# Gate and up products by Strassen's seven block products, with GpSimd making the weight sums

## The chip, the cores and the metric

The kernel runs on one core of a Trainium2 chip, as one program. The metric is the device time of one execution in microseconds. The core's engines run side by side and are ordered by semaphores alone: TensorE (PE, matmuls, with its weight loads as a row of their own), VectorE (DVE), ScalarE (ACT), GpSimd (POOL) and SyncE (SP), whose queue issues the loads from memory. Each engine works through its own list of instructions in order.

## What is computed

Two transformer layers, then one block of another kind, over 512 tokens of width 1024 in float32. Each of the three ends in a gated feed-forward part (FFN) with 2816 hidden features; only that part is touched:

```python
for l in range(DEPTH):                       # 2 layers
    ...                                      # attention; x = x + mix @ w_o[l]
    xn = _rms_norm(x, ffn_norm[l])
    gate, up = jnp.split(xn @ w_gate_up[l], 2, axis=-1)
    x = x + (jax.nn.silu(gate) * up) @ w_down[l]
...                                          # second block, with w_ffn_in, w_ffn_out:
x = x + g2 * _swiglu(_modulate(_rms_norm_2(x, norm2_g[i]), sh2, sc2), w_ffn_in[i], w_ffn_out[i])
```

## The kernel before

**Precision by parts.** Every float32 operand of a large product is split into a rounded high part and the rest, the low part, both in the format that TensorE reads at full rate. A product is three passes: high by high, high by low, low by high. High parts are made by ScalarE copies (`split_high`, line 1865, for weights), low parts by VectorE subtractions (`split_low`, line 2447). All matmuls are issued by one helper, so they carry line 865.

**One FFN** (`ffn`, line 1152). Features are on the partitions. The 2816 hidden features are 22 tiles of 128 (`FT`). For tile q < 22, the weights' columns of gate and up, 1024 x 128 each, are loaded as two transfers of 512 KB into one of two raw buffers, `raws[:, g % 2]` (line 1570); ScalarE copies the 2048 columns to `wH[:, g % 2]`, VectorE subtracts to `wL[:, g % 2]`. TensorE runs 8 contraction tiles x 3 passes for gate into one bank of PSUM, and as many for up into another: 48 matmuls that read 512 columns each. For q from 22 on, 16 halves of the down projection follow: 11 hidden tiles x 3 passes, 33 matmuls of 512 columns, with 1408 weight columns to load and split. The load of piece g waits until the low part of piece g-2 is made (line 1566), so two pieces are on their way at any time.

**Between gate and down** (`scaled_products`, line 2401, for the two layers): VectorE multiplies the gate's bank by the inverse norm (line 2404), ScalarE takes SiLU (line 1890), VectorE multiplies by the up bank (2408), splits the next weights, scales again (2411) and at once splits the hidden tile into `hH` and `hL` (2440, 2441). In the second block the norm is applied ahead of the products and the two scalings fall away (`ffn_products`, ScalarE reads the gate's bank).

**Stream tiles.** While the output projection's eight tiles come out of PSUM, VectorE adds each to `xT`, applies the gain and splits it with ScalarE into `xH`, `xL`, so that the first gate products can follow at once.

**Conditioning.** Beside the two layers' FFNs, GpSimd weighs and folds 64 pieces of `w_ada` of 512 KB (`conditioning`, lines 735 to 749), one for each step q = 0 to 31; SyncE loads each behind the weights of step q+1 (line 1580), TensorE transposes it at the end of step q (`modulation`), ScalarE reads it out.

Of the kernel before, what the change touches and what calls it, by code (L numbers as in the profile page):

```python
# [20 lines left out]
FF = 2816  # L21
# [60 lines left out]
def build(nc, A, out):  # L82
    ctx = ExitStack()
    with ctx:
# [85 lines left out]
        xH = sb("xH", [P, KT, S], FR)  # L170
        xL0 = sb("xL0", [P, KT // 2, S], FR)
        hH = sb("hH", [P, FT, S], FR)
        hL = sb("hL", [P, FT, S], FR)
        xL1 = sb("xL1", [P, KT // 2, S], FR)
        kept = sb("kept", [P, 2048])
        FP = 2 * KT * P
        raws = sb("raws", [P, 2, FP])
        wH = sb("wH", [P, 2, FP], FR)
        wL = sb("wL", [P, 2, FP], FR)
        sb("spare_held", [P, 2, KT * P])  # L180

# [49 lines left out]
        def wo_parts(e):  # L231

            n, home = WO_ROWS * P, WO_HOMES[e]
            a = home * 2 * n if home < 4 else (18816, 6656)[home - 4]
            raw_, parts_ = (ring_flat, ring_parts_flat) if home < 4 else (R, R_parts)
            return [t.rearrange("p (k c) -> p k c", k=WO_ROWS)
                    for t in (raw_[:, a:a + n], parts_[:, a + n:a + 2 * n], parts_[:, a:a + n])]

# [140 lines left out]
        ADA_FIRST, N_ADA = 0, len(ADA) // L  # L379
# [19 lines left out]
        ctx_root, ctx_inverse, ctx_split = sem("ctx_root"), sem("ctx_inverse"), sem("ctx_split")  # L399
        sq_ready, folded = sem("sq_ready"), sem("folded")  # L400
        sums_full, spread_full, inv_copied = sem("sums_full"), sem("spread_full"), sem("inv_copied")
        token_inv_ready, lat_eps_ready = sem("token_inv_ready"), sem("lat_eps_ready")
        gate_full, gate_scaled = sem("gate_full"), sem("gate_scaled")
# [27 lines left out]
        silu_ready, silu_used = sem("silu_ready"), sem("silu_used")  # L431
# [4 lines left out]
        cs_ready, mod_ready = sem("cs_ready"), sem("mod_ready")  # L436
# [204 lines left out]

        ysb = U[:, :, :].rearrange("p a c -> p (a c)")[:, 0:TT * D].rearrange("p (t c) -> p t c", t=TT)
# [5 lines left out]
        def _(pool):  # L648
# [160 lines left out]
            pool.wait_ge(wl_ready, L * NF)  # L809
# [35 lines left out]
            pg.seen[folded] = 2 * L * (KT - 2)  # L845
            fold_squares()


        @block.tensor
        def _(pe):  # L850
# [54 lines left out]
            def stream_sums(l):  # L905

                if l > 0:
                    pe.wait_ge(inv_copied, l)
# [243 lines left out]
            def ffn(l):  # L1152
# [3 lines left out]
                else:  # L1156
                    folded_sums(X(0), X(KT - 1))
                    spread_roots(S)

                def gate_bank(q):  # L1160
                    n = l * FT + q
                    if n >= 2:
                        pe.wait_ge(gate_scaled, n - 1)
                    return A_BANKS[q % 2]
# [11 lines left out]
                xl = lambda k: (xL0 if k < KT // 2 else xL1)[:, k % (KT // 2), :]  # L1176
                for q in range(NF):
                    g = l * NF + q
                    pe.wait_ge(wl_ready, g + 1)
                    if l == L and q == 0:  # L1180
                        w = [[(lambda k, t=t, n=n: t[:, g % 2, (n * KT + k) * P:(n * KT + k + 1) * P]) for t in (wH, wL)] for n in range(2)]
                        banks = [ab.fill(pe), db.fill(pe)]
                        for k in range(KT):
                            pp.more(xn_ready)
                            both = [products(banks[n][:, :], w[n], lambda k: xH[:, k, :], xl, [k], k == 0, k == KT - 1) for n in range(2)]
                        both[0].then_inc(a_full, 1)
                        both[1].then_inc(d_full, 1)
                        f_by.append((d_full, db.n))
                    elif q < FT:
                        for n, b_ in ((0, ab), (1, db)):  # L1190
                            w = [(lambda k, t=t: t[:, g % 2, (n * KT + k) * P:(n * KT + k + 1) * P]) for t in (wH, wL)]
                            deferred = l < L and n == 0
                            bank = gate_bank(q) if deferred else b_.fill(pe)
                            products(bank[:, :], w, lambda k: xH[:, k, :], xl, list(range(KT)), True, True,
                                     (lambda k: pp.more(xn_ready)) if q == 0 and n == 0 else None
                                     ).then_inc(gate_full if deferred else b_.filled, 1)
                            if l < L and q == 0:
                                if n == 0:
                                    stream_sums(l)
                                else:  # L1200
                                    pp.more(diag_ready)
                                    mm(NB[:, :], ones[:, :], dg[:, :], True, True).then_inc(spread_full, 1)
                        f_by.append((d_full, db.n))
# [1641 lines left out]
```

## Time and profile before

| | |
|---|---|
| time, median of 2 | 2747.14 us (2746.83 to 2747.44) |
| the profiled execution | 2746.26 us, of which the span of the profile is 2744.5 |
| TensorE busy | 2597.4 us (95%) |
| VectorE busy | 1413.8 us (52%) |
| ScalarE busy | 1011.3 us (37%) |
| GpSimd busy | 850.8 us (31%) |
| chain that ended last | TensorE 80%, VectorE 11%, ScalarE 5% |
| memory read | 226 MB, 83 GB/s over the span |

A busy share is an average over stages. In the chain's row the shares are of the span, followed back from the last instruction. A matmul's duration in the trace (0.39 us for 512 columns) is its way through the array; matmuls overlap, and what one costs is the distance from its start to the next one's.

### The profile page before, as it was taken

The numbers are of one execution on the slowest core, as the hardware profiler recorded it, in microseconds if no ns is written. First come the engines' busy times: TensorE is split into PE (matmuls) and PEld (weight loads), VectorE is DVE, ScalarE is ACT, GpSimd is POOL, SyncE is SP. The second block draws the span as 40 slices with busy tenths as digits, with TensorE's granted clock in tenths as the row PEclk, the third lists the DMA queues.
The fourth block names the chain that finished last, engine by engine and source line by source line (L and its number), as shares of the span: only waits on it lengthen the run. The fifth ranks groups of instructions, "written<-read, shape, count | busy, mean of one in ns | idle before, by whom it ended". The sixth has DMA issues, their size and how long they took to land.

```text
span 2744.5 us, 35667 instructions
## 1 busy us (share of the span) xinstructions
PE 2597.4 (95%) x13916; PEld 2151.6 (78%) x13916; DVE 1413.8 (52%) x1863; ACT 1011.3 (37%) x1732; POOL 850.8 (31%) x654
## 2 busy tenths in 40 slices
PE   7998999999999988999999899997998999899998
PEld 6976778888899667888888688876876788688887
DVE  2848664454427487654443445557555633534332
ACT  5448722222334487222222344453233200222222
POOL 5467534434435476334444110032000112000000
PEclk9999999999999999999999999998999999999999
DMA  5321034444432100345545121211112234233322
GB/s 127 87 54 23 11 91 130 139 138 139 135 95 88 49 16 11 106 123 147 145 128 155 46 50 47 57 37 46 47 47 54 67 95 123 62 93 92 93 87 82
DMA packets 396711, 230.47 MB, mean 84 GB/s; under 512 B 9744, under 2 KB 392848, under 8 KB 396544
## 3 DMA queue, kind: packets, MB, share of 16 engines
q1 hardware_dynamic: 394608, 226.19, 29.2%
q0 software_dynamic: 1936, 2.00, 0.9%
q8 instruction: 111, 1.82, 0.3%
q14 instruction: 56, 0.46, 0.1%
HBM read 226.07 MB, written 2.10 MB: 83 GB/s over the span
## 4 chain that ended last, share of the span: by engine, by line
PE 80%; DVE 11%; ACT 5%; issue 2%; DMA 1%; POOL 0%; DVEq 0%; SPq 0%; ACTq 0%; POOLq 0%
PE ps L865 70%; PE scores L865 8%; DVE R L2224 1%; PE ps L1009 1%; DVE ring_parts L2500 1%; DVE spare L2234 1%; DMA ring<-in_w_in 1%; DVE wL L2447 1%; DMA R<-in_x 0%; DVE R L2676 0%; ACT R L1731 0%; DVE QK_parts L2214 0%; ACT spare L1726 0%; DVE R L2677 0%; PE scores L937 0%
## 5 line engine op out<-in xcount | busy, mean ns | idle before, releaser
L865 PE MATMUL ps<-xH,wH 128*128 128x512 f32 x1000 | 395.7, 396 | 6.8 <-DVE xL L2420 4.6
L865 PE MATMUL ps<-xH,wL 128*128 128x512 f32 x1000 | 390.8, 391 | 0.0
L865 PE MATMUL ps<-xL,wH 128*128 128x512 f32 x1000 | 390.7, 391 | 0.0
L1865 ACT ACTIVATE wH<-raws 128x2048 fp32r<-128x2048 f32 (+1 forms) x114 | 193.0, 1693 | 465.2 <-PE ps L865 381.4
L865 PE MATMUL ps<-ring_parts,U_parts 128*128 128x256 f32 (+2 forms) x2000 | 328.9, 291 | 27.9 <-DVE ring_parts L2500 14.2
L2447 DVE TENSOR_TENSOR wL<-raws,wH 128x2048 fp32r<-128x2048 f32 (+1 forms) x114 | 237.8, 2086 | 188.6 <-ACT wH L1865 187.2
L865 PEld LDWEIGHTS ps<-ring_parts,U_parts 128*128 128x128 f32 x2000 | 289.9, 197 | 36.0 <-DVE ring_parts L2500 15.4
L865 PE MATMUL ps<-R 128*64 128x128 f32 (+4 forms) x1538 | 224.2, 318 | 31.3 <-DVE R_parts L2245 7.0
L742 POOL TENSOR_TENSOR spare<-spare,cvec 128x1024 f32<-128x1024 f32 x64 | 123.9, 1935 | 400.9 <-DMA spare<-in_w_ada 400.8
L817 POOL CAST ring_parts<-ring 128x2048 fp32r<-128x2048 f32 x34 | 65.6, 1929 | 569.3 <-DMA ring<-in_w_in 500.3
L865 PE MATMUL ps<-U_parts,ring_parts 128*128 128x512 f32 (+2 forms) x768 | 228.2, 386 | 6.7 <-DVE ring_parts L2500 6.7
L865 PEld LDWEIGHTS ps<-R 128*128 128x128 f32 (+1 forms) x1538 | 162.9, 166 | 86.9 <-issue 38.8
L865 PEld LDWEIGHTS ps<-xH,wH 128*128 128x128 f32 x1000 | 188.6, 189 | 52.8 <-issue 5.2
L865 PEld LDWEIGHTS ps<-xH,wL 128*128 128x128 f32 x1000 | 188.6, 189 | 40.1
L865 PEld LDWEIGHTS ps<-xL,wH 128*128 128x128 f32 x1000 | 188.6, 189 | 37.8
L865 PE MATMUL ps<-hH,wH 128*128 128x512 f32 x528 | 208.3, 394 | 0.0
L865 PE MATMUL ps<-hH,wL 128*128 128x512 f32 x528 | 206.0, 390 | 0.0
L865 PE MATMUL ps<-hL,wH 128*128 128x512 f32 x528 | 205.6, 389 | 0.0
L746 POOL TENSOR_TENSOR spare<-spare 128x512 f32<-128x512 f32 (+1 forms) x168 | 170.7, 1016 | 13.2
L865 PEld LDWEIGHTS ps<-U_parts,ring_parts 128*128 128x128 f32 (+1 forms) x768 | 139.8, 186 | 40.7 <-DVE ring_parts L2500 8.1
L712 POOL TENSOR_TENSOR ring_parts<-ring,ring_parts 128x2048 fp32r<-128x2048 f32 (+2 forms) x23 | 99.7, 4337 | 164.8 <-ACT ring_parts L1651 164.5
L865 PE MATMUL ps<-ring_parts 128*128 128x512 f32 (+1 forms) x400 | 137.6, 344 | 0.0
(450 smaller groups left out, 4712.0 us busy)
## 6 DMA issues: line engine op xcount, KB each, us to landing
raws<-in_w_gate_up SPq DMA_DIRECT2D x88, 512.0 KB, 5.2
ring<-in_w_in SPq DMA_DIRECT2D x34, 1024.0 KB, 6.0
spare<-in_w_ada SPq DMA_DIRECT2D x64, 512.0 KB, 3.8
raws<-in_w_down SPq DMA_DIRECT2D x32, 704.0 KB, 5.6
raws<-in_w_ffn_in SPq DMA_DIRECT2D x44, 512.0 KB, 5.1
ring<-in_w_in SPq DMA_DIRECT2D x26, 512.0 KB, 5.4
raws<-in_w_ffn_out SPq DMA_DIRECT2D x16, 704.0 KB, 4.5
ring<-in_w_o SPq DMA_DIRECT2D x12, 448.0 KB, 3.7
```

The source lines that it names most:

```text
L712: pg.do(nc.gpsimd.tensor_tensor(low, slot(i, KT, n_), high.bitcast(F32), ALU.subtract), piece_low)
L742: pg.do(nc.gpsimd.tensor_tensor(w_, w_, bc(cvec[:, :, ADA[a][1]], P, 2), ALU.mult))
L746: pg.do(nc.gpsimd.tensor_tensor(w[:, 0:n_ * P], w[:, 0:n_ * P], w[:, n_ * P:2 * n_ * P], ALU.add), ada_summed if n_ == left else None)
L817: pg.do(nc.gpsimd.tensor_copy(high, raw_), second_high)
L865: return nc.tensor.matmul(o, a, b, start=first, stop=last)
L1009: ins = nc.tensor.transpose(bank[:, s_ * P:(s_ + 1) * P], PX[a % 4][:, c, s_ * P:(s_ + 1) * P], ident[:, :])
L1865: ap.do(f(wH[:, g % 2, 0:n], raws[:, g % 2, 0:n], ACT.Copy), wh_ready)
L2224: vp.do(v.tensor_reduce(nmax[:, n:n + 2], SP[a % 2][:, :, :], AX.X, ALU.max, negate=True), s_max)
L2234: vp.do(v.scalar_tensor_tensor(px[:, 0, :], px[:, 1, :], ratio[:, 0:1], px[:, 0, :], ALU.mult, ALU.add), combined)
L2447: vp.do(v.tensor_tensor(wL[:, g % 2, 0:n], raws[:, g % 2, 0:n], wH[:, g % 2, 0:n].bitcast(F32), ALU.subtract), wl_ready)
L2500: vp.do(v.tensor_tensor(low, raw_, high.bitcast(F32), ALU.subtract), piece_split)
```

## The change

The contraction (1024) is halved, the tokens (512) are halved, and the output side is the pair (gate, up): a 2 x 2 by 2 x 2 block product, done with seven block products (Winograd's form) of 128 x 512 weights by 512 x 256 activations in place of eight. Each block product has 4 contraction tiles x 3 passes, 84 matmuls of 256 columns a hidden tile.

- The weights' blocks A11, A12 (gate), A21, A22 (up, called S3 and A22 when they land) come by four loads of 256 KB into one landing area, `landing`, 3584 columns, of which the loads fill four blocks of 512. GpSimd makes S1, S2, S4 and S3 there by four operations of 512 columns (`weight_sums`). ScalarE copies a first group of four blocks (2048 columns) and a second group of three (1536); VectorE subtracts 2048, then 1024 and 512. The parts are held twice, the landing area once: a tile's loads wait for `lows_made(l, q - 1)`, both low groups of the tile before.
- The activations' sums (T1 to T4) are made by VectorE in the two layers and by GpSimd in the second block (`stream_differences`), and split as before.
- The seven products go to four banks, three pairs of them adding up in place. ScalarE copies product 1 out (`copy_first`); VectorE puts the sums together (`first_sums`, `gate_tile`, `hidden_tile`).
- Hidden tiles are kept whole; they are split all together during the last tile, for want of room (`hidden_high`, `hidden_low`).
- Conditioning moves two steps later (`ADA_FIRST` from 0 to 2), and GpSimd does it between the sums. Some semaphores are merged.

```diff
+        landing = ring_flat[:, 0:7 * QW]
+        FIRST_GROUP, SECOND_GROUP = ("A11", "S3", "S1", "S2"), ("A12", "A22", "S4")
+        def lows_made(l, q):
+            return l * (2 * FT + 2 * KT) + (2 * q + 2 if q < FT else FT + q + 1)
+        H_TURNS = ((0, 7, 4), (7, 12, 7 + 2), (12, 17, 7 + 4), (17, 19, 7 + 5), (19, FT, 7 + 6))
+        PRODUCTS = (("A11", "B11"), ("S1", "T1"), ("S2", "T2"), ("S3", "T3"), ("A12", "B21"), ("S4", "B22"), ("A22", "T4"))
-        ADA_FIRST, N_ADA = 0, len(ADA) // L
+        ADA_FIRST, N_ADA = 2, len(ADA) // L
...
+            def weight_sums(l, j):
+                w = full_part
+                pool.wait_ge(raw_in[0], weights_landed(l, j))
+                for dst, a, b, op in (("S1", "S3", "A22", ALU.add), ("S2", "S1", "A11", ALU.subtract),
+                                      ("S4", "A12", "S2", ALU.subtract), ("S3", "A11", "S3", ALU.subtract)):
+                    pg.do(nc.gpsimd.tensor_tensor(w[dst], w[a], w[b], op), sums_made if dst == "S3" else None)
             def conditioning(l):
                 pool.wait_ge(cs_ready, 1)
+                for j in range(ADA_FIRST + 2):
+                    weight_sums(l, j)
                 for a in range(l * N_ADA, (l + 1) * N_ADA):
...
+                    if a - l * N_ADA + ADA_FIRST + 2 < FT:
+                        weight_sums(l, a - l * N_ADA + ADA_FIRST + 2)
...
+                    for a_, b_, end in ((wh, xh, False), (wh, xl_, False), (wl, xh, i == KH - 1)):
+                        ins = nc.tensor.matmul(o, a_, b_, start=begin, stop=end, skip_group_check=goes_on)
...
+                        pe.wait_ge(wl_ready, lows_made(l, q) - 1)
+                        if q >= 2:
+                            pe.wait_ge(h_made, n - 1)
...
+                        pe.wait_ge(wl_ready, lows_made(l, q))
+                        pe.wait_ge(first_taken, n + 1)
+                        for m in range(4, 7):
+                            if m == 5:
+                                pe.wait_ge(fifth_taken, n + 1)
...
-                    if q >= 2:
-                        sp.wait_ge(wl_ready, g - 1)
+                        if q >= 1:
+                            sp.wait_ge(wl_ready, lows_made(l, q - 1))
+                        for half, gate, up in ((0, "A11", "S3"), (1, "A12", "A22")):
+                            for a, name in enumerate((gate, up)):
+                                sp.dma_start(full_part[name].rearrange("p (k c) -> p k c", k=KH),
...
+            def weights_room(l, j, products_of_two_ago):
+                if j >= 2:
+                    act.wait_ge(quad_full, 7 * (l * FT + j - 2) + products_of_two_ago)
...
+                act.wait_ge(sums_made, l * FT + j + 1)
...
                 for q in range(NF):
                     if q < FT:
+                        if q + 1 < FT:
+                            second_group_high(l, q + 1)
                         else:
+                            split_high(l, FT)
+                        if q > 0:
+                            copy_first(l, q)
+                        if q == 0:
+                            silu(q)
+                        if q + 2 < FT:
+                            first_group_high(l, q + 2)
...
+                        if q > 0:
+                            silu(q)
...
+            def first_group_low(l, j):
+                vp.more(wh_ready)
+                vp.do(v.tensor_tensor(first_low[j % 2], landing[:, 0:4 * QW], first_high[j % 2].bitcast(F32), ALU.subtract), wl_ready)
...
+            def hidden_tile(l, q):
+                dve.wait_ge(quad_full, 7 * (l * FT + q + 1))
+                vp.do(v.tensor_tensor(up_tile[:, 0:TH], quad_banks[l][q][3], partial, ALU.add))
+                if l < L:
+                    vp.do(v.tensor_tensor(up_tile, up_tile, inv, ALU.mult))
+                vp.more(silu_ready)
+                vp.do(v.tensor_tensor(h_full[q], h_full[q], halves(up_tile), ALU.mult), h_made)
...
+                for q in range(FT):
+                    if q > 0:
+                        if q + 1 < FT:
+                            second_group_low(l, q + 1)
...
+                        first_sums(l, q)
...
+                    gate_tile(l, q)
+                    if q + 2 < FT:
+                        first_group_low(l, q + 2)
...
+                    hidden_tile(l, q)
```

## Rows read from the trace of the kernel before

**Rows 1.** The page, part 2: TensorE's busy tenths in 40 slices.

```profile
PE   7998999999999988999999899997998999899998
```

**Rows 2.** Two gate/up windows: PE, PEld, DVE, ACT, POOL busy; clock; DMA share, GB/s.

```profile
480.00:546.00 66.00, 66.00 (x295) 54.30 (x294) 32.90 (x36) 17.53 (x24) 26.31 (x25) 1.00 0.51 143
2400.00:2466.00 66.00, 66.00 (x293) 54.65 (x292) 24.60 (x24) 15.09 (x12) 0.00 (x0) 1.00 0.36 99
```

**Rows 3.** The chain of waits, 480 to 494 us: start, us, what.

```profile
481.74 10.93 PE ps L865 x48
492.67 0.11 PE scores L937
```

**Rows 4.** Timeline, one low part and the next load: start, us, engine, instruction.

```profile
505.73 2.29 DVE L2447 TENSOR_TENSOR wL<-raws,wH 128x2048 fp32r<-128x2048 f32 x1 [1.26 <-ACT wH L1865]
...
508.05 1.00 SPq L1570 DMA_DIRECT2D raws<-in_w_gate_up  x2
```

**Rows 5.** Timeline of TensorE, matmuls of 256 columns, the 24 between two starts.

```profile
155.65 1.84 PE L865 MATMUL ps<-ring_parts,U_parts 128*128 128x256 f32 x14
...
158.53 1.84 PE L865 MATMUL ps<-ring_parts,U_parts 128*128 128x256 f32 x14
```

**Rows 6.** The raw buffers' loads, 2400 to 2466 us: issue (ns), and landing.

```profile
L1570 SPq DMA_DIRECT2D raws<-in_w_ffn_in x12: 367/476/585, 2407.0 to 2461.8; - x12
...
DMA to landing us min/median/max: 3.9/4.6/5.3
```

**Rows 7.** Timeline, GpSimd and VectorE beside each other, at two places.

```profile
404.09 1.91 POOL L742 TENSOR_TENSOR spare<-spare,cvec 128x1024 f32<-128x1024 f32 x1 [26.11 <-DMA spare<-in_w_ada]
404.26 2.02 DVE L2377 TENSOR_SCALAR R<-xT,fg 128x512 f32<-128x512 f32 x1
...
412.05 0.69 DVE L2360 TENSOR_TENSOR xT<-xT,ps 128x512 f32<-128x512 f32 x1
...
2322.85 2.29 DVE L2500 TENSOR_TENSOR R_parts<-R,R_parts 128x2048 fp32r<-128x2048 f32 x1
...
2323.66 2.63 POOL L732 TENSOR_TENSOR U<-U 128x512 f32<-128x512 f32 x1 [2.55 <-ACT U L1659]
2329.14 1.28 POOL L732 TENSOR_TENSOR U<-U 128x512 f32<-128x512 f32 x1 [2.85 <-ACT U L1659]
```

**Rows 8.** Groups by line and form (busy us, mean ns); last a line's min/median/max ns.

```profile
L2447 DVE TENSOR_TENSOR wL<-raws,wH 128x2048 fp32r<-128x2048 f32 x66 | 151.3, 2293 | 77.9 <-ACT wH L1865 77.6
L1865 ACT ACTIVATE wH<-raws 128x2048 fp32r<-128x2048 f32 x66 | 126.6, 1918 | 213.5 <-PE ps L865 212.9 <-ACT rt L1691 0.2 <-ACT R L1894 0.2
L712 POOL TENSOR_TENSOR ring_parts<-ring,ring_parts 128x2048 fp32r<-128x2048 f32 x17 | 79.0, 4652 | 125.8 <-ACT ring_parts L1651 125.4
L2411 DVE TENSOR_TENSOR R<-R 128x512 f32<-128x512 f32 x44 | 31.3, 711 | 1.5
L732 POOL TENSOR_TENSOR U<-U 128x512 f32<-128x512 f32 x6 | 10.5, 1744 | 20.6 <-ACT U L1659 20.6
...
L746 POOL TENSOR_TENSOR spare<-spare x12: 460/735/1295, 478.9 to 514.3; 128x512 f32<-128x512 f32 x4, 128x256 f32<-128x256 f32 x4, 128x128 f32<-128x128 f32 x4
```

**Rows 9.** First gate product, end of the output projection, first down products.

```profile
409.65 0.39 PE L865 MATMUL ps<-xH,wH 128*128 128x512 f32 x1
...
2354.39 0.95 PE L898 MATMUL ps<-ones,U 128*128 128x1 f32 x8
...
L865 PE MATMUL ps<-hH,wH x176: 387/389/477, 658.2 to 780.0; 128*128 128x512 f32 x176
...
L865 PE MATMUL ps<-hH,wH x176: 389/389/481, 2609.2 to 2731.6; 128*128 128x512 f32 x176
```

**Rows 10.** Windows of 8 us: TensorE's granted clock after PE, PEld, DVE, ACT, POOL.

```profile
2346.00:2354.00 8.00, 8.00 (x37) 6.63 (x36) 0.75 (x1) 2.55 (x2) 1.98 (x2) 1.00 0.00 0
2354.00:2362.00 8.00, 4.44 (x21) 2.65 (x19) 4.85 (x6) 2.80 (x3) 0.00 (x0) 0.71 0.36 104
...
1900.00:1908.00 8.00, 0.00 (x0) 0.00 (x0) 7.59 (x12) 2.57 (x3) 1.99 (x1) 0.50 0.17 56
```

More of the change, by code:

```diff
@@ L845, in _ @@
             pg.seen[folded] = 2 * L * (KT - 2)
+            weight_sums(L, 0)
             fold_squares()
+            for k in range(KT):
+                pg.more(tile_made)
+                stream_differences(pg, nc.gpsimd, k)
+            for j in range(1, FT):
+                weight_sums(L, j)
         @block.tensor
@@ L1174, in products @@
                     return ins
-                xl = lambda k: (xL0 if k < KT // 2 else xL1)[:, k % (KT // 2), :]
-                for q in range(NF):
[L1178 to L1203, printed above, removed]
@@ L1208, in ffn @@
                             bank = db.fill(pe)
-                        ins = products(bank[:, :], w, lambda k: hH[:, k, :], lambda k: hL[:, k, :],
+                        ins = products(halves(bank[:, :]), w, lambda k: h_high[k], lambda k: h_low[k],
                                        list(range(a * HK, (a + 1) * HK)), a == 0, a == 1,
@@ new lines, in first_group_low, with second_group_low @@
+            def first_group_low(l, j):
+                vp.more(wh_ready)
+                vp.do(v.tensor_tensor(first_low[j % 2], landing[:, 0:4 * QW], first_high[j % 2].bitcast(F32), ALU.subtract), wl_ready)
+            def second_group_low(l, j):
+                vp.more(wh_ready)
+                high = second_high_[j % 2].bitcast(F32)
+                for n, (a, b) in enumerate(((0, 2), (2, 3))):
+                    vp.do(v.tensor_tensor(second_low_[j % 2][n], landing[:, (4 + a) * QW:(4 + b) * QW], high[:, a * QW:b * QW],
+                                          ALU.subtract), wl_ready if n else None)
@@ new lines, in gate_tile @@
+            def gate_tile(l, q):
+                n = 7 * (l * FT + q)
+                first, fifth, _, _ = quad_banks[l][q]
+                gate = h_full[q]
+                dve.wait_ge(quad_full, n + 5)
+                if l < L:
+                    vp.do(v.tensor_tensor(gate[:, 0, :], first, inv[:, 0:TH], ALU.mult))
+                else:
+                    vp.do(v.tensor_copy(gate[:, 0, :], first))
+                dve.wait_ge(quad_full, n + 6)
+                vp.do(v.tensor_tensor(gate[:, 1, :], fifth, partial, ALU.add), None if l < L else gate_scaled)
+                if l < L:
+                    vp.do(v.tensor_tensor(gate[:, 1, :], gate[:, 1, :], inv[:, TH:S], ALU.mult), gate_scaled)
@@ L2443, in split_low @@
             def split_low(l, q):
-                g = l * NF + q
+                a = (q - FT) % 2
                 vp.more(wh_ready)
-                n = FP if q < FT else HK * P
-                vp.do(v.tensor_tensor(wL[:, g % 2, 0:n], raws[:, g % 2, 0:n], wH[:, g % 2, 0:n].bitcast(F32), ALU.subtract), wl_ready)
-            def ffn_products(l):
-                for j in range(FT):
-                    bank = db.take(dve)
-                    vp.more(silu_ready)
-                    t = PTb[:, 1, :]
-                    vp.do(v.tensor_tensor(t, Pb[:, j % 2, :], bank[:, :], ALU.mult), d_free)
-                    vp.also(silu_used)
-                    split_low(l, j + 2)
-                    split(hH[:, j, :], hL[:, j, :], t, h_ready)
+                vp.do(v.tensor_tensor(down_low[a], down_full[a], down_high[a].bitcast(F32), ALU.subtract), wl_ready)
             def ffn_sums(l, add):
```

342 lines of the change are left out of this document (255 added, 87 removed).

## The prediction

> **What bounds the kernel now.** First the page's slices: TensorE is busy in nine tenths or more of almost every slice [rows 1]. Then the windows of two gate/up stretches: TensorE has no gap in either and its clock is full, while VectorE is busy 33 of 66 us, ScalarE 18 and GpSimd 26 at most [rows 2]. The chain of waits says the same: it goes through 48 TensorE products without a break in 10.93 us, then one 0.11 us transpose, then the next 48 [rows 3]. So a hidden tile costs 11.04 us, 0.227 us a product, and 66 of them (22 tiles, three FFNs) make 729 us. All splitting of weights lies beside that: two raw buffers, two pairs of parts. In the timeline the low part of a tile ends at 508.02 and its buffer's next load is issued at 508.05 [rows 4]; the load has nearly a whole TensorE tile to land before anyone wants it.
>
> **Change, TensorE's side.** A tile becomes 7 products x 4 contraction tiles x 3 passes = 84 matmuls of 256 columns. The trace has such matmuls back to back: 24 of them between 155.65 and 158.53 us, 0.120 us each [rows 5]. 84 x 0.120 = 10.1 us against 10.9: a saving of 0.85 us a tile, 56 us in all, not an eighth, since a 256-column matmul takes 0.120 and not 0.1135 us. If everything else stayed hidden, that would be the result. The down products (512 columns, the two halves in one access pattern) keep their 0.227 us.
>
> **Change, the weights' side.** Here I find the new bound. One landing area replaces two: loads of tile q wait until both low parts of tile q-1 are made, and between landing and low part four GpSimd sums now stand, all before the first copy. VectorE's order also puts the first low part of q, then the hidden tile of q-2, then the second low part of q. Nothing in this loop is doubled, so I add it up once round, from the issue of tile q's loads to that of q+1's:
> - 1 MB in four loads: two loads of 512 KB land 3.9 and 5.3 us after issue, the second issued 0.5 us later [rows 6]. The same bytes: 5.9 us.
> - four GpSimd sums of 128x512: undisturbed such an operation takes 1.28 to 1.30 us [rows 7]; with 0.04 us between them 5.35 us. Bounds: 1.16 (a quarter of the 2048-column one, 4.65) and 1.74 (the mean of a group in which two were blocked) [rows 8].
> - ScalarE copies 2048 columns: 1.92 us; VectorE subtracts 2048: 2.29 us [rows 8].
> - hidden tile of q-2: one 256-column operation from PSUM (no row; by the slope between 2048 and 512 columns, 2.29 [rows 8] and 0.69 [rows 7], it is 0.42), the scaling and the product 0.71 each [rows 8], with gaps 1.95 us. The last FFN has no scaling: 1.2 us.
> - second low part, 1024 and 512 columns: 1.23 (same slope) + 0.69 and gaps = 2.0 us.
> - seven hand-overs between engines of 0.03 to 0.05 us as in [rows 4]: 0.2 us.
> Sum: 5.9 + 5.35 + 1.92 + 2.29 + 1.95 + 2.0 + 0.2 = 19.6 us; last FFN 18.8. ScalarE's way from its first copy on (SiLU, 512 columns, and a second copy of 1536, less than 1.92) is under 2.6 us where VectorE's first low part and hidden tile take 4.2: it hides. A TensorE tile is 10.1 us, so TensorE can't be the bound: it will stand idle about half of each tile. It feels the loop directly, for ScalarE's copy of product 1, which product 5 waits for, is queued behind the second copy of the next tile's weights.
>
> **Contention.** In the first two FFNs GpSimd also weighs conditioning halves (1.91, 1.29, some 0.8 and 0.46 us) [rows 7, 8], now queued right behind each tile's sums, so they run while VectorE makes the low parts. The trace shows the two engines shutting each other out: a GpSimd sum of 1.29 us takes 2.63 beside a VectorE subtraction of two SBUF tiles, a VectorE scaling of 512 columns takes 2.02 and ends 0.28 us after the GpSimd operation beside it; an addition from PSUM (412.05) is not touched [rows 7]. Laying the three conditioning operations left after the first copy into VectorE's five, each alternation costs: 0.8 (what is left of 1.29) + 0.75 + 0.46 = 2.0 us. Bounds 0 and 2.5 (all three in full). It applies to 18 rounds in each of two FFNs. GpSimd's own work, 5.35 + 4.5 = 9.9 us a tile, is under the loop.
>
> **Starts and ends.** Let T be the end of the output projection (409.65, 2354.4) [rows 9]. Before, down products begin at T+248.5 (T+254.8 in the last FFN), their first two halves take 2 x 7.6 us: T+264 and T+270. After, first FFNs: tile 0 loads from T-13.4, is summed and split by T+2.2; its second low part waits for ScalarE behind the stream tile and comes at T+10.5; loads of tile 1 follow, and VectorE has its first low part (5.9 + 5.35 + 1.92 + 2.29 later, T+26), the three sums of tile 0, the root and the second low part: loads of tile 2 at T+30.5. From there 19 rounds to tile 21's loads and one to its low parts: 20 x 19.5 = 390, T+420. There the down weights load (704 KB, so under 5.9; I take 5.0), are copied and split (1408 columns, by the slopes 1.4 and 1.6), and 22 hidden tiles are split in VectorE's queue between the last sums (22 x 0.73 = 16 us, with first sums 1.3, gate 1.3, second down half 1.6, hidden 1.9 us, last copy and product 1.4): 32 us, T+452. With 18 x 2.0 = 36 us contention T+488: +224 us for each of two FFNs. Last FFN: eight tiles' differences run on GpSimd after the norm (about T+8; 4 x 1.3 + 4 x 2.5 us), only then tile 1's sums, so tile 2's loads come at T+41; 20 x 18.75 + 32: T+448, +178 us.
> Smaller: conditioning of the down phase now runs two steps later, and its halves wait for ScalarE behind the last hidden copies; one stall of some 7 us in two FFNs, +14 (0 to 14). TensorE's clock falls in long idle pieces: full in the window before T, 0.71 in the one with 3.6 us idle, 0.50 in one without work [rows 10]. With 10.1 us of slack in a round this mostly hides; I take +15, bounds 0 and 75 (all products at 1.2 GHz, 20.2 us a tile, just above the loop, which adds 28 to 38 us a phase less what contention hides). The next layer's first piece loads one down half later (about -13 us from the end, 6.0 + 1.9 + 4.65 us needed): 0 to 2 us. The stream differences are in the starts. Fewer semaphores: nothing.
> Sum on the profiled span: 2744.5 + 2 x 224 + 178 + 14 + 15 = 3399.5; with the 1.8 us that the profiled execution has around its span (2746.3; the median is 2747.1) 3401: I say 3400.
>
> The Trainium skill (Trainium Kernel Development and Optimization, Best Practices) says to double-buffer so that transfers overlap compute; this change gives that up for the raw weights, and [rows 4] against the loop above agree that this is what costs.
>
> **Rivals.**
> A, forecast: the loop binds, 3400.
> B, faster: a round of the loop turns out below 10.2 us, so TensorE stays gapless: 2747 - 56 = 2691 us. For it speaks that today's splitting is wholly hidden [rows 2]; against, that landing, one copy and one subtraction alone are 5.9 + 1.92 + 2.29 = 10.1 us before any GpSimd sum. It decides at a round of 11.0 us. The no-difference case is the same at 10.8 to 11.9 us.
> C, milder: the loop binds but the conditioning never collides and landing takes 5.0 us (the median 4.6 [rows 6] and an issue): 3400 - 72 - 63 x 0.9 = 3271.
> D, harsher by clock: each idle piece leaves TensorE at 1.2 GHz long enough that products 1 to 7 are late for the loop: 3400 + 60 = 3460; with the GpSimd sums at 1.74 us too, + 60 x 1.8 = 3568. For it, the clock in [rows 10]; against, the slack.
> The Trainium skill (TensorE: Matmul & The Clock Gate, HAM oscillation) describes D's first half: bursts of matmuls between DMA waits run cold each time. The trace shows the drop, not yet in a repeating pattern.
> E, the products don't sum as planned, e.g. 256-column matmuls at 0.15 us in this order: 12.6 us a tile, hidden under the loop: 3400 as well.
>
> **Numbers.** A (with E) 0.66, C 0.15, D 0.15, B 0.02, no difference 0.02. A's own range, its terms' bounds partly compensating, is 3320 to 3480; C and D widen it to 3260 to 3500, with a tenth left on either side. A measurement of this kernel tells 2% from no change. Faster by over 2%: 0.02, within: 0.02, slower: 0.96.
>
> **What would show it.** In the page after: TensorE's busy tenths at about 5 in the gate/up slices; the landing area's loads issued every 19 to 22 us; the chain of waits going DMA, GpSimd sums, ScalarE copy, VectorE, and round again; first low parts of 2.29 us stretched beside conditioning; 256-column matmuls 0.120 us apart within a burst. It is wrong if the loads come every 10 us (B), if VectorE waits for something else than landing and sums, or if TensorE's products take most of 20 us (D).

## The result, and the profile after

The changed kernel takes 3436.57 us (median of 2 runs, 3434.44 to 3438.69) against 2747.14 before: 1.2515 times as long, 95% interval 1.2495 to 1.2535, or +689 us. The profiled execution's span is 3436.9 us against 2744.5.

The page after, busy time by engine, the 40 slices (TensorE's busy tenths, then its granted clock), and the chain that ended last by engine:

```profile
PE 2777.4 (81%) x16296; PEld 2426.9 (71%) x16296; DVE 1754.5 (51%) x2365; ACT 1187.3 (35%) x1930; POOL 1292.8 (38%) x934
...
PE   7989866666799989766666999998998996767688
...
PEclk9999977777899999777777999999999996777799
...
PE 45%; DVE 23%; POOL 10%; DMA 10%; ACT 7%; issue 3%; SPq 3%; ACTq 0%; DVEq 0%; POOLq 0%
```

The slices at 8 and 9 of [rows 1] have become 6 and 7 in the gate/up phases of the three FFNs; the clock's 7s stand in the same places. Windows of two of these stretches (length; PE, PEld, DVE, ACT, POOL busy; clock; DMA share, GB/s), to be read against [rows 2]:

```profile
480.00:800.00 320.00, 205.82 (x1270) 198.99 (x1271) 143.54 (x180) 66.98 (x84) 171.97 (x118) 0.75 0.26 74
2900.00:3200.00 300.00, 208.68 (x1322) 201.56 (x1321) 112.14 (x151) 67.97 (x62) 82.50 (x64) 0.77 0.20 57
```

No engine is full: TensorE is busy 64% of the first window, GpSimd 54%, VectorE 45%, ScalarE 21%, and the DMA engines move 74 GB/s where they moved 143. Where everyone is idle part of the time, the bound is to be looked for in a chain and not in one engine. One round of it stands in the chain of waits (start, us, what), cut to the pieces over 0.3 us:

```profile
592.59 0.37 SPq L1699
...
593.00 0.51 SPq L1699
...
593.55 0.51 SPq L1699
...
594.10 5.47 DMA ring<-in_w_gate_up
...
599.71 1.30 POOL ring L833
...
601.08 1.30 POOL ring L833
...
602.45 1.29 POOL ring L833
...
603.82 1.31 POOL ring L833
...
605.23 1.92 ACT R_parts L2020
...
607.24 3.35 DVE R_parts L2601
...
610.62 0.43 DVE R L2640
...
611.08 0.70 DVE R L2642
...
611.80 0.84 DVE R_front L2644
...
612.67 1.24 DVE R_parts L2607
...
613.93 0.70 DVE R_parts L2607
...
614.65 0.37 SPq L1699
```

It reads: issue and landing 7.0 us, four GpSimd sums 5.4, ScalarE's copy 1.9, first low part 3.35, hidden tile 2.0, second low part 2.0, and the next tile's loads are issued: 22.06 us, with TensorE nowhere in it. Counted from the first low part of one tile to that of the next, over 15 rounds in the middle of each phase, the rounds are 21.7, 21.8 and 19.2 us in the three FFNs, where a tile took 11.04 us before. The round shown has a long landing. Averaged over tiles 3 to 19 of each FFN, hand-overs included, the landing takes 6.8, 6.8 and 6.2 us, the sums 5.5 in all three, the copy 2.0, the first low part 3.34, 3.34 and 2.29, and the rest of VectorE's turn 4.06, 4.06 and 3.20.

Groups by line and form after (busy us, mean ns | idle before), beside [rows 8]:

```profile
L833 POOL TENSOR_TENSOR ring<-ring 128x512 f32<-128x512 f32 x264 | 343.6, 1302 | 781.4 <-DMA ring<-in_w_gate_up 486.2 <-DMA ring<-in_w_ffn_in 279.7
L2601 DVE TENSOR_TENSOR R_parts<-ring,R_parts 128x2048 fp32r<-128x2048 f32 x33 | 96.6, 2927 | 300.4 <-ACT R_parts L2020 300.4
L2020 ACT ACTIVATE R_parts<-ring 128x2048 fp32r<-128x2048 f32 x33 | 63.1, 1912 | 507.7 <-POOL ring L833 491.4 <-PE ps L1293 16.3
```

Each engine of the loop names the one before it as what it waited for: GpSimd the landing, ScalarE GpSimd, VectorE ScalarE. The same 2048-column subtraction went from 2293 ns [rows 8] to a mean of 2927 ns: it takes 3.34 us in the rounds of the first two FFNs and still 2.29 in the last.

### The profile page after: what moved, and what is told of

The parts are those of the page before. It is cut to its first block, busy times and chain, and to the rows that moved or that the text cites. A ratio compares the mean times of both kernels' runs of the same rounds, so it can differ in the third digit from the quotient of the medians.

```text
span 3436.9 us, 42279 instructions
## 1 busy us (share of the span) xinstructions
PE 2777.4 (81%) x16296; PEld 2426.9 (71%) x16296; DVE 1754.5 (51%) x2365; ACT 1187.3 (35%) x1930; POOL 1292.8 (38%) x934
## 4 chain that ended last, share of the span: by engine, by line
PE 45%; DVE 23%; POOL 10%; DMA 10%; ACT 7%; issue 3%; SPq 3%; ACTq 0%; DVEq 0%; POOLq 0%
PE ps L975 36%; POOL ring L833 9%; DMA ring<-in_w_gate_up 6%; PE scores L975 5%; DVE R_parts L2601 3%; DVE ring_parts L2601 3%; DMA ring<-in_w_ffn_in 3%; SPq L1699 3%; DVE R_parts L2607 2%; DVE ring_parts L2607 2%; ACT R_parts L2020 2%; ACT ring_parts L2020 2%; DVE R_front L2644 1%; PE ps L1293 1%; DVE R L2413 1%
## 5 line engine op out<-in xcount | busy, mean ns | idle before, releaser
L1293 PE MATMUL ps<-U_parts,ring_parts 128*128 128x256 f32 x1476 | 429.3, 363 | 274.7 <-ACT R L2006 153.6
L833 POOL TENSOR_TENSOR ring<-ring 128x512 f32<-128x512 f32 x264 | 343.6, 1302 | 781.4 <-DMA ring<-in_w_gate_up 486.2
L1293 PEld LDWEIGHTS ps<-U_parts,ring_parts 128*128 128x128 f32 x1476 | 343.0, 266 | 295.2 <-issue 132.4
L1293 PE MATMUL scores<-U_parts,ring_parts 128*128 128x256 f32 x504 | 160.7, 358 | 237.8 <-ACT R L2006 148.7
L1293 PE MATMUL ps<-R_parts,ring_parts 128*128 128x256 f32 x1200 | 341.6, 334 | 1.4 <-DVE R_parts L2595 1.4
L1293 PEld LDWEIGHTS ps<-R_parts,ring_parts 128*128 128x128 f32 x1200 | 270.3, 246 | 2.7 <-DVE R_parts L2595 2.0
L848 POOL TENSOR_TENSOR spare<-spare 128x512 f32<-128x512 f32 (+2 forms) x164 | 251.8, 1535 | 12.9
L2601 DVE TENSOR_TENSOR R_parts<-ring,R_parts 128x2048 fp32r<-128x2048 f32 x33 | 96.6, 2927 | 300.4 <-ACT R_parts L2020 300.4
L975 PE MATMUL ps<-R_parts,ring_parts 128*128 128x512 f32 x888 | 245.3, 389 | 0.0
L975 PE MATMUL ps<-R_parts 128*128 128x512 f32 x896 | 223.8, 395 | 0.0
L1293 PE MATMUL scores<-U_parts,R_parts 128*128 128x256 f32 x792 | 218.8, 325 | 0.0
```

Source lines behind the costliest of these rows:

```text
L833: pg.do(nc.gpsimd.tensor_tensor(w[dst], w[a], w[b], op), sums_made if dst == "S3" else None)
L975: return nc.tensor.matmul(o, a, b, start=first, stop=last)
L1293: ins = nc.tensor.matmul(o, a_, b_, start=begin, stop=end, skip_group_check=goes_on)
L2601: vp.do(v.tensor_tensor(first_low[j % 2], landing[:, 0:4 * QW], first_high[j % 2].bitcast(F32), ALU.subtract), wl_ready)
```

## Experiments

The theory under test is the prediction's: a serial loop over the landing area sets the time, and each of its steps counts in full. The rivals: TensorE and its clock set it; ScalarE's queue does; the conditioning does; or sharing one landing area costs the time by itself. "Round" is the distance just defined, in the three FFNs.

| kernel | us | ratio to before, 95% | rounds |
|---|---|---|---|
| changed kernel | 3436.6 | 1.2495 to 1.2535 | 21.7, 21.8, 19.2 |
| third pass left out | 3439.5 | 1.2492 to 1.2542 | 21.8, 21.8, 19.2 |
| ScalarE's copy earlier | 3439.9 | 1.2511 to 1.2549 | 21.6, 21.7, 19.2 |
| no conditioning | 3383.0 | 1.2300 to 1.2350 | 20.4, 20.7, 19.3 |
| second low part early | 3360.4 | 1.2213 to 1.2266 | 20.3, 20.3, 18.1 |
| split load waits | 3289.6 | 1.1956 to 1.2008 | 19.1, 19.1, 17.0 |
| the last two together | 3218.7 | 1.1695 to 1.1752 | 17.7, 17.6, 16.3 |
| sums on 2 columns | 3161.5 | 1.1495 to 1.1541 | 17.3, 17.6, 15.0 |
| sums on VectorE, hidden tile ahead | 3297.3 | 1.1974 to 1.2043 | 19.6, 19.6, 17.1 |
| sums on VectorE, hidden tile behind | 3240.7 | 1.1767 to 1.1835 | 19.3, 19.4, 14.6 |
| thin weights' side | 2790.9 | 1.0133 to 1.0196 | 10.2, 10.3, 10.1 |
| before, one landing at a time | 2783.5 | 1.0121 to 1.0157 | |

Before took 2744.7 to 2746.4 us beside them.

**Is it TensorE or its clock?** One of the three passes of every gate/up product is left out:

```diff
-for a_, b_, end in ((wh, xh, False), (wh, xl_, False), (wl, xh, i == KH - 1)):
+for a_, b_, end in ((wh, xh, False), (wh, xl_, i == KH - 1)):
```

> The third pass (low part of the weights by high part of the activations) is left out of all gate and up products: 56 matmuls a tile in place of 84, the weights' low parts are still made. Theory (TensorE is off the loop, clock or no clock): only starts and tails feel it, 0 to 20 us fewer, 3417 to 3437. Rival (TensorE, cold in each burst, takes part in the bound): a third of 10.1 to 20.2 us a tile is 3.4 to 6.7 us, 220 us and more, 3215 or less.

3439.5 us, no difference: a third of the TensorE work of these phases has no price. The timeline of TensorE there shows where the saving went, to the bracketed waits ahead of products 5 and 6 (after, they are 4.81 and 2.87 us at the same two places):

```profile
607.81 0.55 PE L1293 MATMUL ps<-U_parts,ring_parts 128*128 128x256 f32 x1 [7.52 <-ACT R L2006]
613.58 0.58 PE L1293 MATMUL ps<-U_parts,ring_parts 128*128 128x256 f32 x1 [3.73 <-DVE R L2620]
```

The granted clock fell from 0.75 to 0.66 in the window 480 to 800 us (columns as above), and that has no price either:

```profile
480.00:800.00 320.00, 151.40 (x847) 144.65 (x847) 139.95 (x176) 67.42 (x85) 170.32 (x117) 0.66 0.26 74
```

**Is it ScalarE's queue?** ScalarE takes product 1 out of PSUM (L2006) behind the next tile's two copies, and TensorE names this as its longest wait (302 us in all). The copy goes ahead of them, one tile earlier:

```diff
-if q > 0:
-    copy_first(l, q)
 if q == 0:
     silu(q)
+if q + 1 < FT:
+    copy_first(l, q + 1)
```

> ScalarE's copy of product 1 of tile q+1 stands ahead of the first-group copy of tile q+2, no longer behind it and the second-group copy. The table of waits puts 302 us of TensorE's idle time down to that copy. Theory (the loop sets the pace, the copy only fixes where in a round TensorE stands still): TensorE's wait moves to VectorE's sums, the round and the time stay, 3425 to 3440 us. Rival (that wait is a cost of its own): up to 300 us fewer.

3439.9 us, no difference. The wait went where the theory put it: TensorE now waits 547 us in all for VectorE's sums (L2620), where it was 176 us. The largest wait in the list of TensorE's waits was slack.

**The steps of the loop, one at a time.** First the sums: from tile 1 on they work on 2 columns (`w[dst][:, 0:c_]` and the like, `c_ = 2`).

> From tile 1 of each FFN on, the four GpSimd weight sums work on 2 columns in place of 512, so the products use blocks that were not summed; all else is as in the changed kernel. Theory (one loop of landing, sums, copy and low parts sets the pace, 21.7 us a tile in the first two FFNs and 19.2 in the last): each round loses the sums' 5.4 us less some 0.3 that small ones keep, so 5.1 x 63 = 320 us fewer: 3115 us, and the loads' distance falls to some 16.6 us. Rival (TensorE at half clock, 20.2 us a tile, is just behind the loop): the round falls only to about 20, and the time to 3350.

The second low part moves from behind the hidden tile to right behind the first:

```diff
-if q + 1 < FT:
-    second_group_low(l, q + 1)
-else:
+if q + 1 == FT:
...
 first_group_low(l, q + 2)
+second_group_low(l, q + 2)
```

> VectorE makes the second low part of tile q+2 right after the first one and the hidden tile of q after both; nothing is left out. Theory (the hidden tile stands in the loop): a round falls by it, 2.0 us in the first two FFNs (21.7 to 19.7) and 1.2 us in the last, 40 and 20 rounds: some 105 us fewer, 3330 us. Rival (the second low part then waits for ScalarE's second copy, or conditioning collides just as long): under 30 us fewer.

Loads 1 and 2 wait for the first low part alone, loads 3 and 4 for the second:

```diff
-if q >= 1:
-    sp.wait_ge(wl_ready, lows_made(l, q - 1))
 for half, gate, up in ((0, "A11", "S3"), (1, "A12", "A22")):
+    if q >= 1:
+        sp.wait_ge(wl_ready, lows_made(l, q - 1) - 1 + half)
```

> The loads of A11 and A21 of a tile wait for the first low part of the tile before only, the loads of A12 and A22 for both, as now. Nothing is left out. Theory: half of the 1 MB is under way some 4 us earlier, so that from the second low part to the last landing 4.4 us pass (two issues of 0.5 and a landing of 3.9) and not 7.0: 2.6 us a round, 63 rounds, 165 us fewer, 3270 us. Rival (the landing time is latency and not bytes, the last load counts alone): 1.0 us a round, two issues less, 63 us fewer, 3374.

> Both of the two edits before: VectorE's second low part ahead of the hidden tile, and split waits of the loads. Theory: the first half's load now starts only 2 us ahead of the second's, which is as long as its bytes take, so the gains add up: 2.0 + 2.5 us a round in the first two FFNs, 1.2 + 2.5 in the last: 40 x 4.5 + 20 x 3.7 = 254 us fewer, 3183 us. Rival (bytes queue behind each other, the gains overlap): 180 us fewer, 3257.

All four land between theory and rival: -275 us (forecast -322), -76 (-107), -147 (-167), -218 (-254). The first three are nearer to the theory; the last stands in the middle, 36 us from the one and 38 from the other, and doesn't decide by itself. In the last FFN, where nothing runs beside, the sums give 4.2 us a round. From the first sum to ScalarE's copy it was 5.5 us and still is 1.1, since a sum of 2 columns has a fixed part of 0.2 us (195 ns, 252 of them), so 4.4 was due. The early second low part gives 1.1 us there, the 1.2 us of the hidden tile no longer ahead of it. The two orders together give 2.9 us there, for 2.2 and 1.1 apart, and 4.0 in the first FFN, for 2.6 and 1.4: the prices add up, nearly or in full. So the loop is shown by three of its steps, the landing, the sums and the hidden tile. In the first two FFNs some of a gain is lost again because the collision with the conditioning moves. The early second low part was to give 2.0 us and gave 1.4, as the two second low parts then took 2.57 us in place of 1.96. With the short sums the first low part took 2.5 us in place of 3.34, but the operations behind it 5.0 in place of 4.06.

**What does the conditioning cost?** GpSimd's four operations on a conditioning piece work on 16 and 2 columns; the loads of its weights stay.

> GpSimd's four conditioning operations of a piece work on 2 columns each (the sums of the conditioning products are left out); transfers and semaphores stay. Theory (they collide with VectorE's low parts inside the loop): the first two FFNs' round falls from 21.7 to 19.7 us, 38 rounds, and their tails, where the hidden tiles' low parts collide too, by some 8 us each: 90 to 100 us fewer, 3340 us. Rival (the stretched 3.34 us low parts only use up slack): within 15 us of 3437.

-54 us, between the two. The first low part is back at its 2.29 us (groups by line of this kernel), so the collision is real:

```profile
L2601 DVE TENSOR_TENSOR R_parts<-ring,R_parts 128x2048 fp32r<-128x2048 f32 x33 | 75.6, 2292 | 299.9 <-ACT R_parts L2020 299.9
```

But a round falls by 1.1 to 1.3 us, not by 2.0: 1.05 for the first low part and 0.14 for the hidden tile's product. After this cut the first two FFNs still have 20.4 and 20.7 us against 19.3 in the last. Of that, 0.72 is the hidden tile's scaling, which the last FFN doesn't have, and the rest is the landing, which takes 6.8 and 7.0 us on average here and 6.2 in the last FFN. This run keeps the conditioning's loads of 512 KB, issued right behind the tile's. That they slow the tile's is argued, not shown; no run took them away. The tails gained 3.3 and 5.2 us, not 8: the first down product comes 19.3 and 18.0 us after the down weights' first load, for 26.1 and 26.2, but TensorE's wait between the first two down halves grew, from 2.9 to 5.6 us in the first FFN.

**TensorE's side alone.** From tile 2 on each load brings one k-tile of four, and sums, copies and low parts work on 2 columns:

```diff
-w = full_part
+w, c_ = full_part, QW if j < 2 else 2
...
-sp.dma_start(full_part[name].rearrange("p (k c) -> p k c", k=KH),
+sp.dma_start(full_part[name].rearrange("p (k c) -> p k c", k=KH)[:, 0:(KH if q < 2 else 1), :],
```

> From tile 2 of every FFN on, the weights' side is cut to almost nothing: each of a tile's four loads moves one k-tile in place of four, and the four sums, both rounding copies and both low parts work on 2 columns (the products then multiply stale weights). TensorE's products, the hidden tiles and GpSimd's conditioning stay. Theory (the weights' loop is the whole loss; TensorE's side gives what was forecast): tile 1 can be multiplied at T + 27 in the first two FFNs (loads at T + 11.9, then 5.9 + 5.35 + 1.92 + 2.3) and at about T + 42 in the last; 21 tiles of 10.15 us follow, 213 us, so down products begin about 6 us earlier than before in the first two FFNs and 5 us later in the last. With two conditioning stalls of 7 us: 2744.7 - 12 + 5 + 14 = 2752 us, range 2715 to 2780, and rounds of 10.1 to 10.3 us. Rival (the products themselves are slow in this order, by their clock or by 256 columns at 0.15 us): rounds of 12.6 us or more, which is over 2744.7 + 60 x 1.6 = 2840 us.

2790.9 us, above the range's end; the rounds are as forecast. The window of this kernel (columns as above) and one piece of its chain of waits:

```profile
480.00:620.00 140.00, 139.94 (x1167) 139.53 (x1166) 99.56 (x168) 24.59 (x83) 81.35 (x111) 1.00 0.29 80
...
547.77 4.31 PE scores L1293 x36
```

TensorE has no gap, its clock is full, and 36 products take 4.31 us, 0.120 each. Of 689 us lost, all but 45 go with the weights' side. But Strassen's own saving, 0.9 us a tile, doesn't come through either. It is paid at the ends of each phase. Tile 1's first low part ends at 438.57 us, 28 us after the output projection, and TensorE stands still for 5.36 us ahead of tile 0's product 6, whose sums are queued behind that low part. At the other end the last tile's product 6 waits behind VectorE's low parts of hidden tiles, and down products begin at 669.2 us, where before they began at 658.2 [rows 9]:

```profile
664.13 0.58 PE L1293 MATMUL scores<-U_parts,ring_parts 128*128 128x256 f32 x1 [7.23 <-DVE R L2620]
...
680.59 0.41 PE L1047 MATMUL scores<-ident,spare 128*128 128x128 f32 x2 [3.65 <-ACT scores L2103]
```

I had costed the start and the conditioning's stall, and not this tail.

**Is it the single landing area by itself?** The kernel before, with each piece's loads waiting for the low part of the piece just ahead (in the down projection too):

```diff
-if q >= 2:
-    sp.wait_ge(wl_ready, g - 1)
+if q >= 1:
+    sp.wait_ge(wl_ready, g)
```

> The kernel before, but the load of a tile's weights waits until the low part of the tile just before is made, as with one landing area; there are no sums and nothing else changes. The loop is then landing 6.6, copy 1.92 and low part 2.29 us, 10.9 with hand-overs, against TensorE's 11.04 us a tile. Theory (giving up the second landing area alone costs little, the GpSimd sums in the loop make it the bound): within 1% of 2747 us, 2747 to 2775. Rival (the single landing area is the cost by itself): 3 us and more a tile, 2950 or more.

2783.5 us, 8 us beyond the theory's range and far from the rival. Its chain of waits shows why it costs anything:

```profile
494.90 0.37 SPq L1570
...
495.31 5.67 DMA raws<-in_w_gate_up
...
501.09 1.92 ACT wH L1865
...
503.03 3.77 DVE wL L2447
...
506.82 0.37 SPq L1570
```

This loop is 11.9 us in the piece shown, and 11.6 and 11.7 us on average in the first two FFNs, 0.6 above TensorE's tile of 11.04. It is over it only by VectorE's low part: 3.77 us beside GpSimd's conditioning in place of 2.29 [rows 8]. In the last FFN, without conditioning, all 22 low parts take 2.29 us and the window 2400 to 2560 us has TensorE busy for 157.24 of 160. TensorE feels the loop at the end of a tile, at the transpose of a conditioning piece whose load is queued behind the weights': 37 such waits for GpSimd make 17.7 us.

```profile
486.18 0.33 PE L937 MATMUL scores<-ident,spare 128*128 128x128 f32 x1 [0.35 <-POOL spare L746]
```

From the first gate product to the first down product the first two FFNs take 15.9 and 18.2 us longer than before, the last none (245.2 us against 245.3). These 34 us are most of the 38.8; the other 5 weren't followed. A loop costs what it exceeds the bound by, and nothing below that.

**Can the loop be shortened enough?** VectorE makes the sums, right before the first low part; loads wait in halves, and the second low part follows the first. In one version the hidden tile and ScalarE's SiLU also go ahead of the splitting (VectorE's part of that edit is shown), in the other they stay behind:

```diff
 gate_tile(l, q)
+if q < FT - 1:
+    hidden_tile(l, q)
 if q + 2 < FT:
     first_group_low(l, q + 2)
+    second_group_low(l, q + 2)
```

> Nothing is left out. VectorE makes the four sums, right before the first low part, in place of GpSimd; the second low part follows the first at once; each pair of loads waits for its own pair of low parts; the hidden tile and ScalarE's SiLU go ahead of the splitting. Theory (a round is a sum of single steps, so shorter and better overlapped steps shorten it): landing of the second pair of loads 4.3, four VectorE sums of 512 columns 4 x 0.7 = 2.8, copy 1.92, first low part 2.3, second low part 2.0, hand-overs 0.3: 13.6 us, with conditioning beside VectorE's longer row of SBUF operations up to 15.5 in the first two FFNs. Against 21.7 and 19.2 us: 3436.6 - 17 x 2 x (21.7 - 14.5) - 20 x (19.2 - 14) = 3088, with better starts (sums don't wait in GpSimd's queue) some 40 less: 3050 us, range 2980 to 3130. Rival (GpSimd's conditioning shuts VectorE out for as long as the sums took before, so moving them gains little over the same waits and order with GpSimd's sums): rounds of 17 us or more, 3190 us or more.

> Nothing is left out. As the version with VectorE's sums, but the hidden tile and ScalarE's SiLU stand where the change put them, behind the next tile's splitting. That version had rounds of 19.6, 19.6 and 17.1 us; in its last FFN the chain went from VectorE's last gate operation through ScalarE's SiLU and TensorE's product to the hidden tile (2958.60 to 2961.50 us) and only then to the sums. Theory A (moving the hidden tile ahead put TensorE's products into the loop): without it, from the gate operation: sums 2.9, copy 1.9, low parts 2.3 + 2.0, hidden 1.2, first sums 1.8, wait for product 7 2.6, gate 0.4 = 15.3 us in the last FFN, and 2.55 more (as there) = 17.9 in the others: 3297.3 - 2 x 17 x 1.75 - 20 x 1.75 = 3203 us, range 3160 to 3235. Rival B (the hidden tile's place doesn't matter; VectorE's row of operations is too long by itself): the same rounds as there, 3280 to 3310 us.

Both missed. With the hidden tile ahead 3297.3 us: my theory of 3050 is refuted. Behind, 3240.7 us, just above its range. In the last FFN moving it back took the round from 17.1 to 14.6 us (15.3 forecast), so there theory A holds: ahead of the splitting, the hidden tile waits for TensorE's product 7 and ScalarE's SiLU, and puts both into the loop. In the other two FFNs it gave only 0.2 to 0.3 us. Timelines of the last version, the four sums in the first FFN, beside the conditioning, and in the last:

```profile
609.79 5.88 DVE L2597 TENSOR_TENSOR ring<-ring 128x512 f32<-128x512 f32 x4
610.39 1.90 POOL L842 TENSOR_TENSOR spare<-spare,cvec 128x1024 f32<-128x1024 f32 x1 [14.59 <-DMA spare<-in_w_ada]
612.37 3.63 POOL L846 TENSOR_TENSOR spare<-spare 128x512 f32<-128x512 f32 x3
...
2985.89 2.87 DVE L2597 TENSOR_TENSOR ring<-ring 128x512 f32<-128x512 f32 x4
```

Four short VectorE operations next to four GpSimd ones take 5.88 us here, near the longest. Over the rounds of tiles 3 to 19 they take 5.0 and 4.9 us on average in the first two FFNs (4.4 to 6.0) and 2.87 in the last. That is the other rival at 2.1 us a round, and more of it falls on the scaling of the gate half, 1.24 and 1.33 us on average where 0.42 is undisturbed; I had allowed 2.55 for everything. The rest of the 4.8 us between these rounds and the last FFN's is the two scalings that the last FFN doesn't have (0.45 and 0.72 us), some 0.5 us more of waiting for product 7, and 0.25 for ScalarE's second copy. None of these versions beats the kernel before. Why the first two FFNs gained so little from moving the hidden tile back stays open; these versions weren't run without the conditioning.

## Why the prediction was right, point by point

The forecast, 3400 us, was 37 short (1.1%); the runs above bear its mechanism out, and the misses are sizes. That it came so near is in part luck: the landing was put 0.9 us a round too low and the contention 0.8 too high, and 15 us for the clock stood for something that cost nothing.

- **TensorE's tile, 10.1 us:** right (10.1 to 10.3 us in the thin version), and as forecast without any effect.
- **The round without contention, 19.5 and 18.75 us** (its terms add up to 19.6 and 18.85, so 2 us a phase were lost by rounding): 19.2 in the last FFN. Landing was forecast at 5.9 us; in a round there it was 6.06 (loads issued at 3092.50, sums begun at 3098.56 us), 6.2 on average. The sums, 5.35 forecast, took 5.41; the copy 1.91 for 1.92; the hidden tile, in the first two FFNs, 2.0 for 1.95. The landing there was 6.8 us on average (7.1 in the round shown): 0.9 too little, the largest miss of a term of the loop.
- **Contention, +2.0 us a round:** too much. The timeline of the same round:

```profile
605.19 1.90 POOL L844 TENSOR_TENSOR spare<-spare,cvec 128x1024 f32<-128x1024 f32 x1
...
607.17 4.92 POOL L848 TENSOR_TENSOR spare<-spare 128x512 f32<-128x512 f32 x3
...
607.24 3.34 DVE L2601 TENSOR_TENSOR R_parts<-ring,R_parts 128x2048 fp32r<-128x2048 f32 x1 [9.33 <-ACT R_parts L2020]
```

VectorE comes 0.07 us after GpSimd's second operation began and loses 1.05 us (3.34 for 2.29), and later 0.14 on L2644. GpSimd's third then stands behind VectorE's one long instruction, and only the fourth is left for its later ones; L848's three take 4.92 us for 2.5. I had let all of them push VectorE in turn; a single long instruction lets only one by. Without conditioning the round fell by 1.1 to 1.3 us, and that is this term. It compensated for the landing: 21.5 forecast, 21.7 measured. The Trainium skill (SBUF — State Buffer, Who interferes with whom) says that a VectorE instruction with two SBUF inputs contends with a GpSimd instruction that reads SBUF. It calls the shared pair of ports an exclusive lock and says, of VectorE's two-port modes, that whoever issues first has the pair for the whole instruction. The trace agrees on the contention, and here each side did wait for an instruction of the other: 1.05 us lost by the one, 2.4 us by the others.
- **Starts, T + 30.5 and T + 41 for the loads of tile 2:** T + 32.2 and T + 46.1. In the last FFN the first of tile 1's sums begins at 2885.09 us, T + 32, behind the stream differences, and these alternated with VectorE's low parts of them (L2597): the one on L728 takes 1.98 us at 2874.91 and 0.73 at 2880.51.
- **From there to the down weights' loads, 425.5 and 375 us:** 434.6 and 384.8, 9 to 10 us more. In the last FFN that is the rounds' 0.5 us times 20. In the first FFN it is 4 us from 18 rounds and 4 from the last step, from tile 21's loads to the down weights', which took 23.5 us where I had a round without contention, 19.5.
- **The tail, 32 us:** 32.5 in the last FFN, 46.3 in the first. There it failed by 14 us, of which 7 had been counted apart as the conditioning's stall. That stall was 2.9 us. Of the rest 5.9 us are found in the rows below, where the conditioning's operations shut out VectorE in its longest queue. Timeline of the first FFN's tail (L2644 the last product of hidden tile 20, L2721 the low part of down weights, L2650 five low parts of hidden tiles):

```profile
883.67 2.00 POOL L844 TENSOR_TENSOR spare<-spare,cvec 128x1024 f32<-128x1024 f32 x1 [10.21 <-DMA spare<-in_w_ada]
883.94 2.28 DVE L2644 TENSOR_TENSOR R_front<-R_front,R 128x512 f32<-128x512 f32 x1
885.75 3.70 POOL L848 TENSOR_TENSOR spare<-spare 128x512 f32<-128x512 f32 x2
886.25 2.60 DVE L2721 TENSOR_TENSOR ring_parts<-ring,ring_parts 128x1408 fp32r<-128x1408 f32 x1
888.89 6.96 DVE L2650 TENSOR_TENSOR R_parts<-R_front,ring_parts 128x512 fp32r<-128x512 f32 x5
...
897.28 0.58 PE L1293 MATMUL scores<-U_parts,ring_parts 128*128 128x256 f32 x1 [7.01 <-DVE R L2620]
```

Undisturbed, by later rows of the same lines, these take 0.69, 1.62 and 3.6 us: 5.9 us are lost here, in front of the sums that product 6 waits for. Without the conditioning's operations the first down product came 6.8 us sooner behind the down weights' load.

- **By phases:** from T to the end of the second half of down product 0 it was T + 488 forecast and T + 513 measured, in the last FFN T + 448 and T + 463. Against before (T + 264 and T + 270) that is +249 and +193; the spans from T to T give +248.2 and +250.3, and from the last T to the end +193.6, in all 692. Forecast were 224 + 224 + 178 and 29 for stall and clock, 655.
- **The clock, +15 us:** the granted clock averaged 0.75 over 480 to 800 us, a mix of its two levels. After the wait of 4.81 us at 610.29 us TensorE stood at the lower one, 1.2 GHz (0.50 in the window's last columns), with 12 products 0.213 us apart:

```profile
610.30:612.80 2.50, 2.50 (x12) 2.50 (x12) 2.36 (x5) 0.00 (x0) 1.71 (x2) 0.50 0.00 0
```

The Trainium skill (TensorE: Matmul & The Clock Gate, HAM oscillation) describes this for bursts between waits, and the trace agrees. Its price inside the loop was nothing, as the run with two passes shows; rival D is refuted. The 15 us stood in for a miss elsewhere. Their upper bound, 28 to 38 us a phase, doesn't come out of the prediction's own rounds either: 20 x (20.2 - 18.75) is 29 us in the last FFN and 20 x (20.2 - 19.5) 14 in the others. The sign "about 5 tenths" missed for the same reason: at 0.213 us a product TensorE is busy for longer, 205.8 us of 320 where the window's 14.7 rounds of 10.1 us would make 149.
- **Rivals:** B (a round below 10.2 us) would have given 2691; even with the weights' side all but gone it was 2791, so that number was wrong too, since it left out starts and tails. C's landing of 5.0 us didn't come, and the conditioning did collide. E's 0.15 us a product didn't come either: 0.120 in the thin version.
- **"This is what costs", said of double-buffering:** wrong as put. One landing in place of two costs 1.4% in the kernel before. What costs is one landing area together with the sums and VectorE's order, which make its loop twice as long as a TensorE tile. How much a second landing area would give back to the changed kernel wasn't tried.

## What to carry to other kernels

Before an algorithm saves multiplications, write down the loop of the operand that it now has to prepare: from the issue of a buffer's load, through every operation on it, to the next issue, and compare the sum with the time that the multiplications take. Where all engines are idle part of the time, follow the chain of waits round once; the biggest wait in the bound-looking engine's list may be slack. Where two engines shut each other out by the instruction, count how many of the other's instructions fit between yours: a row of short ones loses more than one long one.

## What the runs showed of the hardware

- GpSimd and VectorE took turns by instruction: the conditioning's operations cost one 2048-column VectorE subtraction 1.05 us, and four 512-column ones 2.1 us on average and 3.0 in the round shown.
- A load of 256 KB took 0.37 to 0.84 us to issue (median 0.51) and 2.9 to 5.8 us to land (median 3.9; 60 loads of the first FFN). The sums on a tile's four loads, 1 MB, began 6.2 to 8.0 us after the first issue in the first two FFNs, and 6.0 to 6.5 us after it in the last.
- A GpSimd operation on 2 columns took 0.195 us, one on 512 columns 1.30.
- TensorE came out of a wait of 4.81 us at the lower clock level, 0.213 us a product of 256 columns against 0.120 at the higher one.
